# Phase buffers moved to a multiple of 256 bytes, and 353 matmuls on zeros ahead of the first projection, in a four-layer float32 network on one core

## The chip, the cores and the metric

The kernel runs on 1 core of one Trainium2 chip. The metric is the device time of one execution in microseconds. The kernel before takes 1523.93 us (median of 2 runs, 1523.18 to 1524.68).

## The reference, cut to what matters

The input x is 256 tokens by 1024 features, all in float32. Two networks run one after the other, each of two layers, and each layer is a mixer and a feed-forward part:

```python
# first network, per layer and per sandwich (mixer, then ffn)
shift, scale, gate = silu(c) @ ada_w + ada_b
h = rms_norm(x, g_pre) * (1 + scale) + shift
x = x + gate * rms_norm(fn(h), g_post)       # fn: mixer or swiglu
# mixer of layer 0: h @ hyb_w_in -> pooling and a gated scan (HGRN) -> @ hyb_w_out
# mixer of layer 1: h @ att_w_qkv -> dilated attention -> @ att_w_out
# swiglu: (silu(h @ w_a) * (h @ w_b)) @ w_out, width 2816
# second network, per layer
x = x + mixer(rms_norm(x)) @ w_out           # retention and window attention; then axial attention
x = x + square(relu(rms_norm(x) @ w_up)) @ w_down   # width 4096
```

Nearly all of the arithmetic is products of a 256-row activation with weight matrices that are read once from HBM (273 MB in all).

## The kernel before

Every product of full accuracy is made of three float32r matmuls (`three`, L1384): an operand is split into a rounded part (`hi`) and the rest (`lo`), and hi x hi, hi x lo and lo x hi are summed in one PSUM bank. Weights come in loads of 1 MB from the SyncE queue into `raw`, a ring of 6 slots. Each load is split in two halves of 128x1024. For each half ScalarE writes the rounded part to `whi` (L422) and VectorE the rest to `wlo` (L837), each a ring of 4. TensorE then runs the 24 or 48 matmuls of a half and so frees it. Its matmul instructions all go through `mm` (L1382); a weight load (PEld in the profile) goes with each.

There are three kinds of matmuls that matter here:

- `proj` of kind B and `up`: the stationary operand is a 128x128 piece of `whi` or `wlo`, the moving one 256 columns of `hhi` or `hlo`. The profile writes them `ps<-hhi,whi ... 128x256`, moving operand first.
- `proj` of kind A, and `down` for the output projections: stationary is a piece of `hhi`, `hlo`, `yhi3` or `ylo3`, moving are 512 columns of `whi` or `wlo` (`ps<-whi,hhi ... 128x512`).
- `down` in the feed-forward parts: the same, with the stationary operand a piece of `hidhi1`, `hidlo1` (first network) or `hidhi2`, `hidlo2` (second). The profile writes both pairs `hidhi` and `hidlo`.

SBUF is given out by nested stacks. First come buffers that live through the kernel (`raw`, `whi`, `wlo`, `x`, `hhi`, `hlo`, `cols`, `ident`, `ones`, ..., `small`). Behind them begin the phase buffers, sets that use the same space at different times: `ada_ring`, `acc_a` and the rest of the first network; `tmp2`, `hidhi2`, ...; `f3`, `dist`, ..., `yhi3`, `ylo3`, `qkhi`, `vhi`. In the built program the address of `raw`, `whi`, `wlo`, `hhi` and `hlo` leaves 128 when divided by 256; that of `ident` leaves 0; that of the first phase buffer, of `hidhi1`, `hidlo1`, `hidhi2` and `hidlo2` leaves 224; that of `yhi3`, `ylo3`, `qkhi` and `vhi` leaves 128, since a buffer of 32 bytes (`sinkt`) stands between them and their stack's start.

The start of the kernel, which the change touches: SyncE loads eight 1 MB pieces of `ada_w`; VectorE multiplies them with silu(c) into `acc_a` (`ada_first`, L862 and L864). TensorE runs four small matmuls on `vtab` and `voh` (bias tables) and waits for ScalarE's four copies of them (L571, L573). Then it sums `acc_a` over partitions with `ones` (`sum_cols`), transposes the normalised x (`turn`, L1491) and sums the rest. VectorE turns the sums into scale and shift (`mod_cols`, L878 to L880), makes `h` from the transposes (L936), ScalarE rounds it to `hhi` (L497), VectorE writes `hlo` (L923), and with this the first projection (`hyb_in`) begins. ScalarE's queue has the four copies of the tables ahead of its first weight splits (`split`, L422).

During `hyb_in` VectorE also works through further pieces of `ada_w`, which GpSimd's queue loads into `ada_ring`, two slots of 1 MB (L347; used at L848 and L851). A slot is loaded again once its four pieces are used. After `hyb_in` comes the scan, in eight levels (`for lv in range(NM)`): for each level TensorE waits for VectorE's masked copy of the level two before (`hg_masked`, L1065), runs `keep_warm(4)` (four products of `ident` with itself, 8 instructions), waits for VectorE's next factors (`hg_step`, L1077 to L1079) and ScalarE's copies (`hg_copied`, L625, L626), and runs 8 score products.

```python
def keep_warm(n, bank):
    for _ in range(n):
        mm(ps[:, bank, 0:P], ident[:, :], ident[:, :])
```

Of the kernel before, what the change touches and what calls it, by code (L numbers as in the profile page):

```python
# [18 lines left out]
F32 = mybir.dt.float32  # L19
F32R = mybir.dt.float32r  # L20
# [4 lines left out]
P = 128  # L25
# [54 lines left out]
even_in nr_sq nr_ssq nr_ln nr_r nr_done rp_rot rp_done  # L80
dec_step dec_ready rt_sig rt_s rt_p rt_o rt_sq rt_ssq rt_ln rt_r rt_y rt_hi rt_lo
sw_s sw_z sw_e sw_pn sw_t sw_tc sw_tl sw_o qkv_hi qkv_lo sw_sink sw_hi sw_lo
out_done dve_step act_step one_ready
""".split()


def program(nc, t):

    with ExitStack() as ctx:
        s = {name: ctx.enter_context(nc.semaphore(name)) for name in SEMS}  # L90
# [4 lines left out]
        def sb(stack, name, shape, dt=F32):  # L95
            return stack.enter_context(nc.sbuf_tensor(name, shape, dt))

        ps = ctx.enter_context(nc.psum_tensor("ps", [P, 8, 512], F32))
        raw = sb(ctx, "raw", [P, RAW, 2 * HALF])
        whi = sb(ctx, "whi", [P, 4, HALF], F32R)  # L100
# [9 lines left out]
        sc = sb(ctx, "sc", [P, KD])  # L110
        stat = sb(ctx, "stat", [P, 16])
        small = sb(ctx, "small", [P, 6, 16])


        with ExitStack() as first:
            ada_ring = sb(first, "ada_ring", [P, 2, 4, 512])
            acc_a = sb(first, "acc_a", [P, 6 * 512])
            gg = sb(first, "gg", [P, 2, D])
            grow = sb(first, "grow", [P, D])
            with ExitStack() as r:  # L120
                xn1 = sb(r, "xn1", [P, 2, D])
                h321 = sb(r, "h321", [P, 2, 512])
                vtab = sb(r, "vtab", [33, 24 + 8])
                voh = sb(r, "voh", [33, 3 * VLEN_DIL + VLEN_SWA])
                vrow = sb(r, "vrow", [8, 3 * VLEN_DIL + VLEN_SWA])
            with ExitStack() as r:
                tmp1 = sb(r, "tmp1", [P, 2, 512])
                hid1 = sb(r, "hid1", [P, 2, 512])
                acc_b = sb(r, "acc_b", [P, 2 * 512])
                hidhi1 = sb(r, "hidhi1", [P, 2, 512], F32R)  # L130
                hidlo1 = sb(r, "hidlo1", [P, 2, 512], F32R)
            with ExitStack() as r:
                f1 = sb(r, "f1", [P, 12, S])
                tok1 = sb(r, "tok1", [P, 2, 1024])
                bandqk = sb(r, "bandqk", [P, 2048])
                att1 = sb(r, "att1", [P, 8, P])
                att1o = sb(r, "att1o", [P, 4, P])
                tot2 = sb(r, "tot2", [P, 512])
                masks = sb(r, "masks", [P, NM, P])
                pooled = sb(r, "pooled", [P, 4, S])  # L140
                sq1 = sb(r, "sq1", [P, 4, S])
                poolw = sb(r, "poolw", [P, 4, P])
                y1 = sb(r, "y1", [P, 8, S])
            with ExitStack() as r:
                f2 = sb(r, "f2", [P, 24, S])
                tok2 = sb(r, "tok2", [P, 2, 1536])
                dbias = sb(r, "dbias", [P, 3, DG, S])
                prob2 = sb(r, "prob2", [P, 2, 9 * P])
                pt2 = sb(r, "pt2", [P, 9 * P])
# [188 lines left out]
        def _(pool):  # L338
# [19 lines left out]
                pool.dma_start(grow[:, :], row_of(t["norm_post"][j // 2, j % 2], D)).then_inc(s["grow_in"], 16)  # L358

            SHIFT_SCALE, GATE = [0, 512, 1024, 1536], [2048, 2560]  # L360
            pool.wait_ge(s["ada_used"], 4)
            ada_blocks(0, [(0, n) for n in GATE])
            bias_row(0)
# [457 lines left out]
        def _(dve):  # L821
# [185 lines left out]
                    body(g, 0, SPLITS.get(g, range(4)))  # L1007


            V.memset(ones[:, :], 1.0)  # L1010
            V.memset(shcol[:, :, :], 0.0)
            V.memset(small[:, 5, :], EPS).then_inc(s["one_ready"], 1)
# [367 lines left out]
        def _(pe):  # L1380
            def mm(out, lhsT, rhs, first=True, last=True):
                return pe.matmul(out, lhsT, rhs, start=first, stop=last, skip_group_check=True)  # L1382
# [165 lines left out]
                    body(g)  # L1548


            pe.wait_ge(s["const_in"], 48)
            pe.wait_ge(s["one_ready"], 1)
            for g in range(DG):
# [396 lines left out]
```

## Time and profile before

| what | value |
|---|---|
| median of 2 runs | 1523.93 us (1523.18 to 1524.68) |
| span of the profiled execution, first to last instruction | 1521.2 us |
| median less span | 2.7 us |
| TensorE busy in that span | 1416.0 us (93%), 9162 matmuls |
| VectorE, ScalarE busy | 933.2 us (61%), 706.3 us (46%) |
| mean granted TensorE clock | 0.969 of full speed |
| moved by DMA | 275.55 MB, 181 GB/s in the mean |

The profile gives the profiled execution by its span; its own time isn't listed apart, so what lies around the span is taken as median less span. Times in the rows are microseconds from the span's start. The busy time of a matmul is longer than its share of the engine, because matmuls overlap: what a matmul costs in a row of matmuls is the distance from its start to the start of the next.

### The profile page before, as it was taken

The numbers are of one execution on the slowest core, as the hardware profiler recorded it, in microseconds if no ns is written. First come the engines' busy times: TensorE is split into PE (matmuls) and PEld (weight loads), VectorE is DVE, ScalarE is ACT, GpSimd is POOL, SyncE is SP. The second block draws the span as 40 slices with busy tenths as digits, with TensorE's granted clock in tenths as the row PEclk, the third lists the DMA queues.
The fourth block names the chain that finished last, engine by engine and source line by source line (L and its number), as shares of the span: only waits on it lengthen the run. The fifth ranks groups of instructions, "written<-read, shape, count | busy, mean of one in ns | idle before, by whom it ended". The sixth has DMA issues, their size and how long they took to land.

```text
span 1521.2 us, 22829 instructions
## 1 busy us (share of the span) xinstructions
PE 1416.0 (93%) x9162; PEld 1281.7 (84%) x9162; DVE 933.2 (61%) x1155; ACT 706.3 (46%) x956; POOL 49.2 (3%) x75
## 2 busy tenths in 40 slices
PE   4898999999999998999989997899999997899998
PEld 2787899998898778999988995779998895798997
DVE  6878768875786546454465647654445548554444
ACT  2554444444444334444454646445554545445553
POOL 0100000000110000000001000000000000000000
PEclk9999899999999799999999997999999998999999
DMA  9983568985598302555546540254555540335650
GB/s 358 386 307 128 180 221 302 313 268 194 204 352 304 97 11 84 193 173 187 191 140 205 166 167 20 62 166 144 189 193 175 167 166 28 111 124 181 192 165 28
DMA packets 146049, 275.55 MB, mean 181 GB/s; under 512 B 4695, under 2 KB 83311, under 8 KB 145848
## 3 DMA queue, kind: packets, MB, share of 16 engines
q1 hardware_dynamic: 130592, 219.17, 43.1%
q0 software_dynamic: 13872, 52.05, 10.4%
q10 hardware_dynamic: 1512, 3.31, 0.6%
q8 instruction: 53, 0.87, 0.2%
q14 instruction: 20, 0.16, 0.0%
HBM read 273.40 MB, written 1.10 MB: 180 GB/s over the span
## 4 chain that ended last, share of the span: by engine, by line
PE 82%; DVE 10%; ACT 3%; DMA 3%; issue 2%; SPq 0%; DVEq 0%; ACTq 0%
PE ps L1382 80%; DVE h L936 1%; DMA raw<-in_hyb_w_in 1%; DVE wlo L837 1%; DMA ada_ring<-in_ada_w 1%; DMA raw<-in_ada_w 1%; DVE acc_a L851 1%; PE ps L1491 1%; ACT whi L422 1%; ACT pt L667 1%; DVE hlo L923 1%; DVE x L905 1%; DVE h L903 0%; ACT xn L480 0%; PE ps L1662 0%
## 5 line engine op out<-in xcount | busy, mean ns | idle before, releaser
L837 DVE TENSOR_TENSOR wlo<-raw,whi 128x1024 fp32r<-128x1024 f32 x400 | 486.3, 1224 | 443.0 <-ACT whi L422 442.6
L422 ACT CAST whi<-raw 128x1024 fp32r<-128x1024 f32 x400 | 419.3, 1050 | 606.2 <-PE ps L1382 586.9
L1382 PE MATMUL ps<-hhi,whi 128*128 128x256 f32 x1792 | 508.1, 284 | 8.1 <-DVE hlo L923 8.1
L1382 PE MATMUL ps<-hhi,wlo 128*128 128x256 f32 x1792 | 507.0, 283 | 0.0
L1382 PE MATMUL ps<-hlo,whi 128*128 128x256 f32 x1792 | 506.9, 283 | 0.0
L1382 PEld LDWEIGHTS ps<-hhi,whi 128*128 128x128 f32 x1792 | 343.3, 192 | 12.4 <-issue 10.3
L1382 PEld LDWEIGHTS ps<-hlo,whi 128*128 128x128 f32 x1792 | 343.3, 192 | 2.2 <-issue 0.2
L1382 PEld LDWEIGHTS ps<-hhi,wlo 128*128 128x128 f32 x1792 | 343.4, 192 | 0.0
L1382 PE MATMUL ps<-whi,hidhi 128*128 128x512 f32 x432 | 171.4, 397 | 0.0
L1382 PE MATMUL ps<-wlo,hidhi 128*128 128x512 f32 x432 | 171.3, 396 | 0.0
L1382 PE MATMUL ps<-whi,hidlo 128*128 128x512 f32 x432 | 171.0, 396 | 0.0
L1382 PE MATMUL ps<-whi,hhi 128*128 128x512 f32 (+1 forms) x256 | 99.0, 387 | 8.6 <-DVE hlo L923 5.2
L851 DVE SCALAR_TENSOR_TENSOR acc_a<-ada_ring,sc,acc_a 128x512 f32<-128x512 f32 (+1 forms) x126 | 94.7, 752 | 9.3 <-DMA ada_ring<-in_ada_w 4.6
L1382 PEld LDWEIGHTS ps<-whi,hidlo 128*128 128x128 f32 x432 | 81.3, 188 | 19.7
L1382 PE MATMUL ps<-whi,hlo 128*128 128x512 f32 (+1 forms) x256 | 97.0, 379 | 0.0
L1382 PE MATMUL ps<-wlo,hhi 128*128 128x512 f32 (+1 forms) x256 | 97.0, 379 | 0.0
L1382 PEld LDWEIGHTS ps<-whi,hidhi 128*128 128x128 f32 x432 | 81.5, 189 | 17.7 <-issue 0.2
L1382 PEld LDWEIGHTS ps<-wlo,hidhi 128*128 128x128 f32 x432 | 81.3, 188 | 17.7 <-issue 0.2
L1382 PE MATMUL ps<-ident 128*128 128x128 f32 x488 | 77.3, 314 | 6.7 <-DVE att L1065 6.6
L1382 PEld LDWEIGHTS ps<-ident 128*128 128x128 f32 x488 | 72.2, 228 | 9.0 <-DVE att L1065 7.5
L1382 PEld LDWEIGHTS ps<-whi,hhi 128*128 128x128 f32 x256 | 48.7, 190 | 19.3 <-issue 7.7
L1382 PEld LDWEIGHTS ps<-wlo,hhi 128*128 128x128 f32 x256 | 48.8, 191 | 9.3 <-issue 0.7
(213 smaller groups left out, 1281.0 us busy)
## 6 DMA issues: line engine op xcount, KB each, us to landing
raw<-in_ffn_w_in SPq DMA_DIRECT2D x44, 1024.0 KB, 5.3
ada_ring<-in_ada_w POOLq DMA_DIRECT2D x40, 1024.0 KB, 6.8
raw<-in_w_mlp_up SPq DMA_DIRECT2D x32, 1024.0 KB, 5.5
raw<-in_w_mlp_down SPq DMA_DIRECT2D x32, 1024.0 KB, 5.0
raw<-in_ffn_w_out SPq DMA_DIRECT2D x22, 1024.0 KB, 5.0
raw<-in_att_w_qkv SPq DMA_DIRECT2D x18, 1024.0 KB, 6.0
raw<-in_w_in_even SPq DMA_DIRECT2D x18, 1024.0 KB, 5.1
raw<-in_hyb_w_in SPq DMA_DIRECT2D x10, 1024.0 KB, 15.0
```

The lines of the kernel that those rows point to most:

```text
L422: A.copy(whi[:, H % 4, :], raw[:, slot(n), h * HALF:(h + 1) * HALF]).then_inc(s["hi_ready"], 1)
L667: A.copy(pt2[:, a:a + n], flat(bank)[:, 0:n] if tt else ps[:, 5, 0:n]).then_inc(s["dl_tc"], 1)
L837: V.tensor_tensor(wlo[:, H % 4, :], raw[:, slot(n), h * HALF:(h + 1) * HALF], whi[:, H % 4, :].bitcast(F32), ALU.subtract).then_inc(s["lo_ ...
L851: ins = V.scalar_tensor_tensor(out=out, in0=ada_ring[:, kh, kk, :], scalar=sc[:, k:k + 1], in1=out, op0=ALU.mult, op1=ALU.add)
L905: V.scalar_tensor_tensor(out=x[:, tt, :], in0=h, scalar=stat[:, 2 + tt:3 + tt], in1=x[:, tt, :], op0=ALU.mult, op1=ALU.add).then_inc(s["x_ ...
L923: V.tensor_tensor(hlo[:, 2 * q:2 * q + 2, :].rearrange("p a b -> p (a b)"), h32[:, q % 2, :], hhi[:, 2 * q:2 * q + 2, :].rearrange("p a b ...
L936: ins = V.tensor_scalar(h32[:, q % 2, kk * S:(kk + 1) * S], ps[:, q, kk * S:(kk + 1) * S], scol[:, j, k:k + 1], shcol[:, j, k:k + 1], ALU. ...
L1382: return pe.matmul(out, lhsT, rhs, start=first, stop=last, skip_group_check=True)
L1491: m = pe.transpose(ps[:, k // 2, (k % 2) * S + tt * P:(k % 2) * S + (tt + 1) * P], xn[:, tt, k * P:(k + 1) * P], ident[:, :])
```

## The change

Three things are done.

1. An unused buffer of 32 bytes (`pad1`) stands behind `small`. Every phase buffer moves up by 32 bytes. In the built program the first phase buffer, `hidhi1`, `hidlo1`, `hidhi2`, `hidlo2`, `f1` to `f3` and `tok1` to `tok3` now leave 0 when divided by 256. `yhi3`, `ylo3`, `qkhi` and `vhi` go from 128 to 160. `raw`, `whi`, `wlo`, `hhi`, `hlo` and `ident` stay where they are.
2. VectorE clears 1024 columns of `whi`, all 2048 of `hhi` and half of a new buffer `warm` (3072 of 6144 columns, at an address that leaves 128) ahead of its other work; GpSimd clears the other half of `warm` ahead of its first wait.
3. TensorE waits for both and runs, ahead of the table matmuls, 25 sets of float32r matmuls on these zeros: one set of 40 and 24 of 12, each with another offset of the stationary operand (in elements of 4 bytes), of the moving operand, of their width or of their number of PSUM banks. Each set ends with a matmul of 64 columns.

```diff
         small = sb(ctx, "small", [P, 6, 16])
+        sb(ctx, "pad1", [P, 8])
...
                 vrow = sb(r, "vrow", [8, 3 * VLEN_DIL + VLEN_SWA])
+                sb(r, "pad2", [P, 64])
+                warm = sb(r, "warm", [P, 6144], F32R)
...
             SHIFT_SCALE, GATE = [0, 512, 1024, 1536], [2048, 2560]
+            pool.memset(warm[:, 3072:6144].bitcast(F32), 0.0).then_inc(s["warm_ready"], 1)
             pool.wait_ge(s["ada_used"], 4)
...
+            V.memset(whi[:, 0, :].bitcast(F32), 0.0)
+            V.memset(hhi[:, :, :].bitcast(F32), 0.0)
+            V.memset(warm[:, 0:3072].bitcast(F32), 0.0).then_inc(s["warm_ready"], 1)
             V.memset(ones[:, :], 1.0)
...
+            pe.wait_ge(s["warm_ready"], 2)
+            hw, ww = hhi[:, :, :].rearrange("p a b -> p (a b)"), whi[:, 0, :]
+            def warm_up(n, a, b, width, outs):
+                for i in range(n):
+                    o = outs[i % len(outs)]
+                    mm(ps[:, o[0], o[1]:o[1] + width], a[i % len(a)], b[i % len(b)][:, 0:width])
+                mm(ps[:, 3, 0:64], ww[:, 0:128], hw[:, 0:64])
...
+            def SS(off):
+                return [at(ww, 128 * i + off, 128) for i in range(7)]
+            def HH(off, n=256):
+                return [at(hw, n * i + off, n) for i in range(3)]
+            W8 = [at(warm, 128 * i, 128) for i in range(8)]
+            W5 = [at(warm, 2048 + 512 * i, 512) for i in range(4)]
+            warm_up(40, SS(0), HH(0), 256, one)
...
+            warm_up(12, SS(96), HH(0), 256, four)
...
+            warm_up(12, SS(96), HH(96, 512), 512, four)
...
             pe.wait_ge(s["const_in"], 48)
```

TensorE's instructions at the program's start, before (`vtab` and `voh` are the bias tables, `ones` with `acc_a` the column sums, `xn1` the normalised x):

```order
L1382 MATMUL ps<-voh,vtab 8x384 x3
L1382 MATMUL ps<-voh,vtab 8x512
L1382 MATMUL ps<-ones,acc_a 128x1 x8
L1491 MATMUL ps<-ident,xn1 128x128 x16
L1382 MATMUL ps<-ones,acc_a 128x1 x8
L1382 MATMUL ps<-whi,hhi 128x512
```

The same place of the changed kernel, the first sets and the last two with what follows (the sets between them are left out):

```order
L1389 MATMUL ps<-hhi,whi 128x256 x40
L1389 MATMUL ps<-hhi,whi 128x64
L1389 MATMUL ps<-hhi,whi 128x256 x12
...
L1389 MATMUL ps<-hhi,warm 128x128 x12
L1389 MATMUL ps<-hhi,whi 128x64
L1389 MATMUL ps<-voh,vtab 8x384 x3
L1389 MATMUL ps<-voh,vtab 8x512
L1389 MATMUL ps<-ones,acc_a 128x1 x8
```

Of the added matmuls 244 are 256 columns wide (40 and 17 sets of 12), 72 are 512 wide, 12 are 128 wide and 25 are 64 wide. They stand ahead of the first thing that TensorE did, and nothing else moved on it.

VectorE's first instructions in the changed kernel (in the one before they begin with the third row from the end of these, the clearing of `ones`):

```order
L1014 MEMSET whi 128x1024
L1015 MEMSET hhi 128x2048
L1016 MEMSET warm 128x3072
L1017 MEMSET ones 128x128
L1018 MEMSET shcol 128x64
L1019 MEMSET small 128x16
```

The three new rows stand ahead of the one that releases ScalarE's first norms (`one_ready`) and of the first use of `ada_w`. On the other engines the order of the instructions is the same, but for GpSimd's one clearing.

## Rows read from the trace of the kernel before

**Rows 1.** The page: busy time, and the chain that ended last.

```profile
PE 1416.0 (93%) x9162; PEld 1281.7 (84%) x9162; DVE 933.2 (61%) x1155; ACT 706.3 (46%) x956; POOL 49.2 (3%) x75
PE 82%; DVE 10%; ACT 3%; DMA 3%; issue 2%; SPq 0%; DVEq 0%; ACTq 0%
```

**Rows 2.** Timeline, TensorE from the start: start, length, what, idle before.

```profile
13.99 5.71 PE L1382 MATMUL ps<-voh,vtab 33*8 33x384 f32 x8 [13.99 <-DMA voh<-in_voh]
20.37 3.72 PE L1382 MATMUL ps<-ones,acc_a 128*128 128x1 f32 x16 [0.67 <-ACT vrow L573]
25.89 3.68 PE L1491 MATMUL ps<-ident,xn 128*128 128x128 f32 x16 [1.81 <-DVE xn L914]
44.29 0.77 PE L1382 MATMUL ps<-whi,hhi 128*128 128x512 f32 x1 [5.25 <-DVE hlo L923]
44.86 0.63 PE L1382 MATMUL ps<-wlo,hhi 128*128 128x512 f32 x1
...
48.27 0.52 PE L1382 MATMUL ps<-whi,hhi 128*128 128x512 f32 x1
```

**Rows 3.** Timeline, VectorE and ScalarE from the start.

```profile
0.84 0.17 DVE L1010 MEMSET ones<- 128x128 f32 x1 [0.84 <-PEq L1937]
6.59 0.49 DVE L862 TENSOR_SCALAR acc_a<-raw,sc 128x512 f32<-128x512 f32 x1 [1.48 <-DMA raw<-in_ada_w]
12.69 3.12 DVE L864 SCALAR_TENSOR_TENSOR acc_a<-raw,sc,acc_a 128x512 f32<-128x512 f32 x4 [3.24 <-DMA raw<-in_ada_w]
19.74 0.58 ACT L573 COPY vrow<-ps 8x512 f32<-8x512 f32 x1 [1.24 <-PE ps L1382]
41.18 0.16 DVE L878 TENSOR_TENSOR shcol<-ps,cols 128x8 f32<-128x8 f32 x1
103.50 0.91 DVE L1053 MEMSET att<- 128x1024 f32 x1 [0.16 <-issue]
```

**Rows 4.** Timeline, TensorE: a `down`'s 1st matmul, what follows its 24th, and the 29th after.

```profile
209.76 0.39 PE L1382 MATMUL ps<-whi,hidhi 128*128 128x512 f32 x1
...
215.37 0.28 PE L1382 MATMUL ps<-hhi,whi 128*128 128x256 f32 x1
...
218.84 0.28 PE L1382 MATMUL ps<-hhi,wlo 128*128 128x256 f32 x1
```

**Rows 5.** Timeline, TensorE: 24 matmuls of the output projection on `yhi3` and `ylo3`.

```profile
991.04 0.39 PE L1382 MATMUL ps<-whi,yhi 128*128 128x512 f32 x1
...
996.48 0.39 PE L1382 MATMUL ps<-whi,yhi 128*128 128x512 f32 x1
```

**Rows 6.** Groups by line and shape: count, busy time and mean ns.

```profile
L1382 PE MATMUL ps<-whi,hidhi 128*128 128x512 f32 x432 | 171.4, 397 | 0.0
L1382 PE MATMUL ps<-whi,yhi 128*128 128x512 f32 x32 | 12.4, 389 | 0.0
```

**Rows 7.** Timeline, VectorE, ScalarE and TensorE, 86 to 124 us.

```profile
86.92 0.49 DVE L848 TENSOR_SCALAR acc_a<-ada_ring,sc 128x512 f32<-128x512 f32 x1 [4.12 <-DMA ada_ring<-in_ada_w]
92.07 3.11 DVE L851 SCALAR_TENSOR_TENSOR acc_a<-ada_ring,sc,acc_a 128x512 f32<-128x512 f32 x4 [2.30 <-DMA ada_ring<-in_ada_w]
113.90 0.66 ACT L625 COPY pooled<-bandqk 128x512 f32<-128x512 f32 x1
118.16 2.08 PE L1382 MATMUL ps<-ident 128*128 128x128 f32 x8 [5.84 <-DVE att L1065]
120.03 3.62 PE L1382 MATMUL ps<-pooled,sq 128*128 128x128 f32 x16
124.44 1.95 PE L1382 MATMUL ps<-bandqk 128*128 128x128 f32 x16
```

**Rows 8.** Busy time by stretch: PE, PEld, DVE, ACT, POOL, then clock, DMA share, GB/s.

```profile
80.00:90.00 10.00, 10.00 (x48) 8.50 (x48) 4.64 (x6) 7.83 (x8) 0.00 (x0) 1.00 1.03 399
118.00:124.00 6.00, 5.84 (x29) 5.84 (x30) 3.17 (x6) 1.39 (x3) 0.00 (x0) 0.53 0.70 231
124.00:130.00 6.00, 5.33 (x46) 4.95 (x44) 6.00 (x9) 2.49 (x5) 0.00 (x0) 1.00 0.00 0
```

More of the change, by code:

```diff
@@ L82 @@
 sw_s sw_z sw_e sw_pn sw_t sw_tc sw_tl sw_o qkv_hi qkv_lo sw_sink sw_hi sw_lo
-out_done dve_step act_step one_ready
+out_done dve_step act_step one_ready warm_ready
 """.split()
@@ L1548, in mlp, with at @@
                     body(g)
+            pe.wait_ge(s["warm_ready"], 2)
[5 more added lines that the diff above has]
+                mm(ps[:, 3, 0:64], ww[:, 0:128], hw[:, 0:64])
+            def at(src, off, n):
+                return src[:, off:off + n]
+            one, two, four = [(0, 0)], [(0, 0), (1, 0)], [(0, 0), (1, 0), (2, 0), (3, 0)]
+            def SS(off):
[5 more added lines that the diff above has]
+            warm_up(40, SS(0), HH(0), 256, one)
+            warm_up(12, SS(0), HH(0), 256, one)
+            warm_up(12, SS(0), HH(0), 256, four)
+            warm_up(12, SS(0), HH(0)[:1], 256, four)
+            warm_up(12, SS(0)[:1], HH(0), 256, four)
+            warm_up(12, SS(96), HH(0), 256, four)
+            warm_up(12, SS(32), HH(0), 256, four)
+            warm_up(12, SS(16), HH(0), 256, four)
+            warm_up(12, SS(8), HH(0), 256, four)
+            warm_up(12, SS(4), HH(0), 256, four)
+            warm_up(12, SS(2), HH(0), 256, four)
+            warm_up(12, SS(96), HH(96), 256, four)
+            warm_up(12, SS(96), HH(32), 256, four)
+            warm_up(12, SS(96), HH(16), 256, four)
+            warm_up(12, SS(96), HH(8), 256, four)
+            warm_up(12, SS(96), HH(4), 256, four)
+            warm_up(12, SS(96), HH(0, 512), 512, four)
+            warm_up(12, SS(96), HH(96, 512), 512, four)
+            warm_up(12, SS(8), HH(0, 512), 512, four)
+            warm_up(12, SS(96), W5, 512, four)
+            warm_up(12, W8, W5, 512, four)
+            warm_up(12, W8, HH(96), 256, four)
+            warm_up(12, W8, [w[:, 0:256] for w in W5], 256, four)
+            warm_up(12, SS(96)[:1], HH(96, 512)[:1], 512, four)
+            warm_up(12, W8, HH(96), 128, four)
             pe.wait_ge(s["const_in"], 48)
```

## The prediction

> **What bounds the kernel now.** I read the page first: TensorE is busy for 93% of the span and stands for 82% of the chain that ended last [rows 1]. So a microsecond that TensorE gains or loses anywhere in its steady stages is one of the kernel's. Then the timeline of the first 50 us [rows 2, 3]: TensorE's real work begins only at 44.29; before it runs 56 small matmuls and waits for `ada_w` and VectorE. That is where the new matmuls are put, so the question is how much of them fits there. Then the distance between matmul starts in steady stretches, by operand [rows 4 to 6], since the move of the buffers can change nothing but that. Last the stretch up to 124 us, where VectorE and DMA and not TensorE set the pace for a while [rows 7, 8].
>
> **The pace of matmuls by operand.** In a feed-forward `down`, 24 matmuls of 512 columns take 215.37 - 209.76 = 5.61 us, 234 ns each; stationary is `hidhi` or `hidlo`, at 224 over a multiple of 256 [rows 4]. In the output projection 24 matmuls with the same moving buffers, banks and order take 996.48 - 991.04 = 5.44 us, 227 ns each; stationary is `yhi3` or `ylo3`, at 128 [rows 5]. The one difference that I see is the stationary operand's address. It even shows in the busy times, 397 ns against 389 [rows 6]. The 256-wide ones with both operands at 128 take 218.84 - 215.37 = 3.47 us for 29 [rows 4], 120 ns.
>
> **Part 1, the move by 32 bytes.** `hidhi` stands in 432 + 432 matmuls and `hidlo` in 432: 1296 in all (one of three rows with the same count stands in [rows 6]). They go from 224 to 0. No row has a float32r matmul with its stationary operand at 0. If 0 is as good as 128, each gains 5.61/24 - 5.44/24 = 7.1 ns: 1296 x 7.1 = 9.2 us. The bounds: the gain may be nothing, and it may be larger, for even at 227 ns a matmul is 14 ns above its 512 columns at 2.4 GHz (213 ns); all of that gone would be 1296 x 21 = 27 us. On the other side a relation of 0 to the moving operand's 128 could be worse than 224 to 128; from the nearest rows I give that the same 7 ns, 9 us. I take -9.2, the row that I have. `yhi3` and `ylo3` go from 128 to 160, in 96 matmuls (3 x 32): if 160 is as bad as 224, +0.7 us. The rest (`qkhi`, `vhi`, VectorE's and ScalarE's operands) I cost at nothing; those matmuls stand among waits on other engines.
>
> The Trainium skill (SBUF — State Buffer, Specifications) gives lines of 16 bytes as what costs when crossed. Both 224 and 0 are multiples of 16, so by that rule the move would be worth nothing; the pair 234 and 227 ns speaks against it, as both of those addresses are multiples too. It is the first rival below. The same skill (TensorE: Matmul & The Clock Gate, Back-to-back issue gap) gives N/2.4 + 2.5 ns for a warm matmul, 216 ns at 512, which no float32r row here reaches; by it the upper bound would be 1296 x 18 = 23 us.
>
> **Part 2, the clearing.** VectorE's 1024 columns of zeros took 0.91 us [rows 3], so 6144 columns are 5.4 us, and it is done at 0.84 + 5.4 = 6.3. Its first `ada_w` piece then starts at about 8 and not 6.59; the wait of 3.24 us before 12.69 [rows 3] swallows this. GpSimd's 3072 columns lie beside it; no row shows its clearing at this size, between 2.7 us (VectorE's rate) and, as an estimate, three times that, 8 us. Its first DMA waited for `ada_used` until 22 us anyway. TensorE starts its sets at 6.5 (up to 8.5).
>
> **Part 3, the sets.** Cold, a 512-wide matmul took 0.426 us (44.86 to 48.27, eight of them) [rows 2], so a 256-wide one is 0.213. The clock rose about 4 us after the projection's start, for the matmul at 48.27 is the first shorter one (0.52). I take 4 us cold here too (19 matmuls). The other 225 of 256 columns: 225 x 0.120 = 27.0. 72 of 512 at 0.227 to 0.234: 16.6. The 37 of 128 or 64 columns are not shown in float32r; between 0.06 us each (columns alone) and 0.21 (cold), I take 0.11, about a weight load: 4.1. Sum 4 + 27.0 + 16.6 + 4.1 = 51.7 us (bounds 46 to 60), to 58.2. Nothing hides beneath it: all of TensorE's start work is queued behind. And ScalarE's first splits stand behind its copies of the tables, which wait for TensorE.
>
> Behind the sets all inputs have landed, and the clock is up. Table matmuls 5.71 us at half clock [rows 2], now 2.9; ScalarE's last copy 0.6 [rows 3]; 16 sums, 16 transposes and 16 sums (8 and 8) at half of 3.7 each [rows 2]: 5.5. Together 9.0, to 67.2. Then from the scale and shift (41.18, rows 3) to the first projection (44.29) 3.1, and 0.3 for the hand-over: 70.6. ScalarE's first four splits run during the sums. **The projection starts 26.3 us later.**
>
> **What comes back.** (a) The projection's first 4.0 us ran at 0.426 instead of 0.227 us: 1.9 us lost before. With TensorE idle for only 3 us and not 5.25 beforehand it should start warm: -1.9 (bounds 0 and -1.9). (b) In the kernel before VectorE waited 4.12 + 2.30 us for `ada_ring`, whose DMAs stood among the weight loads [rows 7] while the queues moved 399 GB/s at full share [rows 8]. VectorE then was late for the scan: TensorE idled 5.84 us before 118.16, and its clock was 0.53 in the 6 us behind [rows 8], so that the 24 matmuls (8 from 118.16, 16 from 120.03, end 123.65) took twice as long as at full clock. After the change the two `ada_ring` loads and six weight loads have landed long before the projection, so the DMA queues are empty when the next are issued. What is late next is ScalarE: its copies for level 1 (113.90, done 115.1 with the second) release level 2, which before began its 16 products at 120.03 and cold. I reckon level 3 (124.44) comes 5 us earlier relative to the projection. Bounds 0 (VectorE late anyway) and -6.4 (all its wait). -5.0.
>
> **Sum** against the profiled span of 1521.2: + 26.3 - 1.9 - 5.0 - 9.2 + 0.7 = + 10.9, to 1532.1. Median less span was 2.7 us, so the time is 1534.8; I say 1534.5.
>
> **Rivals.**
> 1. *The new address of the hidden buffers is worth nothing* (the change doesn't do what it says): what slows them is their relation to the moving operand at 128, and 0 is no better than 224. For it: no row shows a stationary operand at 0. Against: 128 is good, and 0 is the rounder number. Then 26.3 - 6.9 = + 19.4 and no loss on `yhi3`: 1543.
> 2. *0 is better than 128.* The 14 ns above the columns, which `whi` and `hhi` pay at 128, fall away with the stationary operand at 0. For it: those 14 ns ask for a cause, and the stationary address has been seen to move the pace. Against: `whi` as moving operand stays at 128, and may be what costs them. Then 1296 x 21 = 27 in place of 9.2: + 10.9 - 18 = - 7: 1517; half of it 1526.
> 3. *The sets run at half clock throughout, and the kernel is slower by more than 2%* (2% is 30.5 us, about what a measurement of this kernel can tell from no change). Zeros in both operands might not count as work, or the clock may rise late. Then the sets take 244 x 0.213 + 72 x 0.427 + 37 x 0.11 = 86.8 us, 35 more, the small matmuls behind them 8 more: 1534.5 + 43 = 1577. It decides from where the sets take over 51.7 + 20 = 72 us. Against it: `ident` holds zeros in all but one of 128 places, and the clock was 1.0 from 124 to 130 us, where `keep_warm` is a third of the matmuls [rows 8]. A GpSimd clearing of over 25 us would have the same end.
>
> **How the numbers follow.** Forecast 0.57; rival 1 0.20; rival 2 0.15; rival 3 0.08. Cases 1 and 2 with the bounds of the start (- 4 to + 10) and of what comes back (0 to - 8.3) span 1517 to 1553; the range is 1519 to 1553 and leaves out rival 3 and the end of rival 2. Faster by over 2% needs 41 us less than forecast, which no bound gives: 0.01. Slower by over 2% (above 1554.4) is rival 3 and the sum of all bad ends: 0.09. The rest, within 2%: 0.90.
>
> **What would show it.** The first weight split after the sets and the first projection at 70 to 71 us; the sets ending at 58; matmuls on `whi` and `hidhi` at 227 ns and not 234 (24 in 5.44 us), those on `yhi3` at 234; 256-wide ones unchanged at 120; VectorE without a wait for `ada_ring` in the projection, and a gap of TensorE before level 2 of the scan of 2 us and not 5.84. A set that takes over 4 us cold, a pace of 234 or of 215 on `hidhi`, or a gap that stays would each show its own step wrong.

## The result: 1549.87 us, slower by 1.7%

The changed kernel takes 1549.87 us (median of 2 runs, 1549.83 to 1549.9) where the kernel before takes 1523.93: a ratio of 1.0171, interval 1.0141 to 1.02. That is 25.9 us more; the forecast was 10.6 more. The measured time lies inside the predicted range, but the forecast has less than half of the loss. The profiled execution has a span of 1548.1 us and a mean granted clock of 0.971.

The page of the changed kernel, the two lines that answer to [rows 1]:

```profile
PE 1455.6 (94%) x9515; PEld 1321.4 (85%) x9515; DVE 938.8 (61%) x1158; ACT 705.5 (46%) x956; POOL 51.9 (3%) x76
PE 82%; DVE 11%; ACT 4%; issue 2%; DMA 1%; POOL 0%; DVEq 0%; ACTq 0%
```

TensorE has 353 more matmuls and 39.6 us more busy time, and it is as much of the chain as before. DMA's share of the chain fell from 3% to 1%: this is the start, where `ada_w` is no longer waited for.

The timeline of TensorE's start in the changed kernel (start, length, what, idle before), which answers to [rows 2]; the projection's first matmul is the one at 74.20:

```profile
7.35 38.37 PE L1389 MATMUL ps<-hhi,whi 128*128 128x256 f32 x275 [7.35 <-DVE warm L1016]
...
58.81 2.96 PE L1389 MATMUL ps<-voh,vtab 33*8 33x384 f32 x8
62.43 3.58 PE L1389 MATMUL ps<-ones,acc_a 128*128 128x1 f32 x16 [0.66 <-ACT vrow L577]
65.87 3.49 PE L1498 MATMUL ps<-ident,xn 128*128 128x128 f32 x16
69.20 1.84 PE L1389 MATMUL ps<-ones,acc_a 128*128 128x1 f32 x16
74.20 0.77 PE L1389 MATMUL ps<-whi,hhi 128*128 128x512 f32 x1 [3.16 <-DVE hlo L927]
...
79.03 0.52 PE L1389 MATMUL ps<-whi,hlo 128*128 128x512 f32 x1
```

The sets fill 7.35 to 58.81 us. The first of them run at half clock: behind the very first the starts stand 213 ns apart up to 11.0 us, 3.7 us in all, and then 116 to 121 ns. (The trace's record of the clock begins only there.) Then the 16 first sums and the 16 transposes take 3.4 us each, nearly as long as at the start of the kernel before, though nothing but a gap of 0.66 us separates them from 51 us of dense work; only the last 16 sums run at full pace. The projection starts at 74.20 and not at 44.29, 29.9 us later. Its first matmuls stand 0.43 us apart again: the first shorter one is at 79.03.

The busy time by stretch shows why (PE, PEld, DVE, ACT and POOL busy, granted clock, DMA share, GB/s):

```profile
62.50:69.30 6.80, 6.80 (x34) 6.80 (x34) 2.36 (x2) 3.88 (x4) 0.00 (x0) 0.52 0.29 60
74.20:79.10 4.90, 4.90 (x12) 3.88 (x13) 4.70 (x8) 2.18 (x4) 0.00 (x0) 0.50 0.22 59
```

In both stretches TensorE is busy without a gap and is granted 0.5 of its clock (1.2 of 2.4 GHz).

The next view is VectorE's timeline at the scan's inputs, and then TensorE's at levels 2 and 3; it answers to [rows 7]:

```profile
114.81 0.49 DVE L852 TENSOR_SCALAR acc_a<-ada_ring,sc 128x512 f32<-128x512 f32 x1 [1.71 <-DMA ada_ring<-in_ada_w]
119.82 3.12 DVE L855 SCALAR_TENSOR_TENSOR acc_a<-ada_ring,sc,acc_a 128x512 f32<-128x512 f32 x4 [2.15 <-DMA ada_ring<-in_ada_w]
```

```profile
145.90 1.16 PE L1389 MATMUL ps<-ident 128*128 128x128 f32 x8 [3.45 <-DVE att L1072]
146.89 1.95 PE L1389 MATMUL ps<-pooled,sq 128*128 128x128 f32 x16
149.63 1.95 PE L1389 MATMUL ps<-bandqk 128*128 128x128 f32 x16
```

VectorE still waits for `ada_ring`, but 3.9 us and not 6.4. TensorE idles 3.45 us before level 2 and not 5.84, and its 8 and 16 matmuls run at full clock (1.16 and 1.95 us, before 2.08 and 3.62). Level 3 starts 25.2 us later than in [rows 7]: of the 29.9 that the start cost and the 0.5 that the projection's cold stretch is longer, 5.2 came back. How much of this is the change's doing is taken up below, with the prediction's term.

Last, the pace. The timeline of TensorE in a feed-forward `down` of the changed kernel (24 matmuls between the two rows, as in [rows 4]), and in the output projection (24 between the rows, as in [rows 5]):

```profile
235.32 0.39 PE L1389 MATMUL ps<-whi,hidhi 128*128 128x512 f32 x1
...
240.90 0.28 PE L1389 MATMUL ps<-hhi,whi 128*128 128x256 f32 x1
...
1017.48 0.39 PE L1389 MATMUL ps<-whi,yhi 128*128 128x512 f32 x1
...
1023.07 0.40 PE L1389 MATMUL ps<-whi,yhi 128*128 128x512 f32 x1
```

The hidden buffers at 0 give 5.58/24 = 232.5 ns, not the 227 that was forecast (before 234). `yhi3` and `ylo3` at 160 give 5.59/24 = 232.9 ns where they had 227. So the address mattered in both places, and 0 is not a good one. The group's mean busy time says it more weakly, 395 ns where [rows 6] has 397:

```profile
L1389 PE MATMUL ps<-whi,hidhi 128*128 128x512 f32 x432 | 170.7, 395 | 0.0
```

### The profile page after: what moved, and what is told of

It is laid out like the page before. It is cut to its first block, busy times and chain, and to the rows that moved or that the text cites. A ratio compares the mean times of both kernels' runs of the same rounds, so it can differ in the third digit from the quotient of the medians.

```text
span 1548.1 us, 23539 instructions
## 1 busy us (share of the span) xinstructions
PE 1455.6 (94%) x9515; PEld 1321.4 (85%) x9515; DVE 938.8 (61%) x1158; ACT 705.5 (46%) x956; POOL 51.9 (3%) x76
## 4 chain that ended last, share of the span: by engine, by line
PE 82%; DVE 11%; ACT 4%; issue 2%; DMA 1%; POOL 0%; DVEq 0%; ACTq 0%
PE ps L1389 81%; DVE h L940 1%; DVE wlo L841 1%; DVE acc_a L855 1%; PE ps L1498 1%; DMA ada_ring<-in_ada_w 1%; ACT whi L426 1%; DVE x L909 1%; DVE hlo L927 1%; DVE h L907 1%; ACT pt L671 1%; ACT xn L484 0%; PE ps L1716 0%; DVE small L1306 0%; ACT rs L454 0%
## 5 line engine op out<-in xcount | busy, mean ns | idle before, releaser
L1389 PE MATMUL ps<-hhi,whi 128*128 128x256 f32 (+2 forms) x2085 | 551.5, 287 | 20.8 <-DVE hlo L927 12.9
L1389 PEld LDWEIGHTS ps<-hhi,whi 128*128 128x128 f32 x2085 | 384.2, 193 | 27.2 <-issue 15.6
L1389 PE MATMUL ps<-ident 128*128 128x128 f32 x488 | 71.3, 297 | 4.3 <-DVE att L1072 4.2
L1389 PEld LDWEIGHTS ps<-ident 128*128 128x128 f32 x488 | 65.9, 211 | 6.6 <-DVE att L1072 5.1
```

## The experiments

Theory A through all of them: what sets the pace of a float32r matmul is the *difference* of the stationary and the moving operand's addresses modulo 256, and not the stationary operand's own. The hidden buffers had the difference 224 - 128 = 96 and got 0 - 128, which is 128. The good difference for 512 columns would be 0. In all kernels the whole reference is computed; they differ in where buffers lie and in matmuls on zeros. "Before" is the kernel before on the same chip.

### The two halves of the change apart

The move alone:

```diff
# the kernel before
+        sb(ctx, "pad1", [P, 8])
```

> The kernel before with the 32-byte move alone, no clearing and no matmuls on zeros. Theory A (what counts is the stationary operand's address relative to the moving one's, and only an equal remainder by 256 gives 227 ns at 512 columns): in the changed kernel hidhi at 0 against whi at 128 ran at about 232.6 ns, so 1296 x 1.6 ns = 2 us are gained and 96 x 6 ns = 0.6 us lost: 1.4 us faster, about 1522.5. Rival B (the move costs time through VectorE, ScalarE or DMA on the phase buffers, and this is part of the 26 us): slower than 1524, by 5 us or more. The forecast on record would have had it at 1515.4.

Measured: 1520.19 us (10 runs) against 1524.39; ratio 0.9975, interval 0.9965 to 0.9984. The pace on the hidden buffers is 232.3 ns in the mean and on `yhi3` 233. The move is a small gain, 4.2 us, more than the 1.6 of the paces (1296 x 1.7 ns less 96 x 6). The spans of the two profiled executions differ by 2.3. What the gain holds beyond the paces stays open; the ten runs go from 1518.83 us at a mean granted clock of 0.974 to 1523.26 at 0.965.

The sets alone:

```diff
# the changed kernel
-        sb(ctx, "pad1", [P, 8])
```

> The changed kernel without the 32-byte buffer: the matmuls on zeros and the clearing alone. Theory A: 29.9 us later at the first projection, about 3 to 5 us back at the scan, nothing from the move: 1549.9 + 1.4 = 1551, 27 us over before. Rival B: 1545 or less. The first projection starts at 74.2 in either.

Measured: 1556.45 us (4 runs) against 1524.39; ratio 1.0209, interval 1.0189 to 1.0229. Expected was +27, measured +32: a miss of 5 us. The projection starts at 74.70, as expected; all of the sums and transposes but the last few run at half clock. The mean granted clock of the trace is 0.963, where the whole change has 0.971, and of the 7.6 us between the two spans the paces explain 1.6. Why the clock is lower in this kernel was not tried. With the move's -4.2 the two halves sum to +27.9, and the whole change measured +25.9. So the loss is the sets', and its centre is the start. Each half carries some microseconds that neither account explains.

### Theory A: the difference of the addresses

In the kernel before, the hidden buffers are put at 128 over a multiple of 256, where the moving operand is too:

```diff
# the kernel before
+                sb(r, "padh1", [P, 40])
                 hidhi1 = sb(r, ...
...
+            sb(r, "padh2", [P, 40])
             hidhi2 = sb(r, ...
```

> The kernel before with 160 bytes ahead of hidhi1 and hidhi2 alone, so that the hidden buffers leave 128, as whi and wlo do. Theory A: 1296 matmuls from 234.2 to 226.7 ns, 9.7 us faster: 1514.2. Rival C (the hidden matmuls are slow from something else than their address, such as the engine's other traffic in the feed-forward parts): stays at 234 or 232 ns, 1522 to 1524.

Measured: 1516.26 us (4 runs), ratio 0.9953, interval 0.9936 to 0.9969; 8.1 us faster, which is what the prediction had put down for the move. The same place as [rows 4], 24 matmuls in the timeline of TensorE:

```profile
208.50 0.40 PE L1384 MATMUL ps<-whi,hidhi 128*128 128x512 f32 x1
...
213.97 0.28 PE L1384 MATMUL ps<-hhi,whi 128*128 128x256 f32 x1
```

5.47/24 = 227.9 ns: 128 is good for these buffers and 0 is not. This alone doesn't tell the own address from the difference, as only the stationary operand was moved. A kernel that measures the pace by itself replaces the sets with 16 sets of 21, in which the stationary operand's offset goes through 0, 32, ..., 224 bytes while the moving one stays:

```diff
# the changed kernel, in place of the 24 sets of 12
+            for off in (0, 8, 16, 24, 32, 40, 48, 56):
+                warm_up(21, SS(off), HH(0), 256, four)
+            for off in (0, 8, 16, 24, 32, 40, 48, 56):
+                warm_up(21, SS(off), HH(0, 512), 512, four)
```

> The changed kernel with other sets: 40 of 256 columns, then 8 sets of 21 of 256 and 8 of 512 columns, with the stationary operand 0, 32, 64, 96, 128, 160, 192 and 224 bytes past the moving one by the remainder of 256, which stays at 128. Theory A: at 512 columns 227 ns at 0, 233 to 234 at 32, 96, 128; at 256 columns 120 at 0 and 113 at 64, as in the changed kernel's sets; unknown are 160, 192, 224 and 512 columns at 64. If the law is symmetrical, 192 is as 64 and 224 as 32; if it goes by 128, 192 is as 64 and 128 as 0, which the changed kernel already speaks against.

Measured (median distance of starts in a set, ns; difference is stationary less moving, modulo 256 bytes):

| difference | 0 | 32 | 64 | 96 | 128 | 160 | 192 | 224 |
|---|---|---|---|---|---|---|---|---|
| 256 columns | 120 | 118 | 113.5 | 117 | 120 | 120 | 118 | 118 |
| 512 columns | 227 | 233 | 233 | 233 | 232 | 232 | 229 | 234 |

The timeline of TensorE in this kernel, cut to pieces of single sets: 256 columns at the differences 0 and 64, 512 columns at 0 and 32:

```profile
15.28 1.84 PE L1389 MATMUL ps<-hhi,whi 128*128 128x256 f32 x14
...
20.25 1.86 PE L1389 MATMUL ps<-hhi,whi 128*128 128x256 f32 x15
...
37.00 2.67 PE L1389 MATMUL ps<-hhi,whi 128*128 128x512 f32 x11
...
41.69 2.96 PE L1389 MATMUL ps<-hhi,whi 128*128 128x512 f32 x12
```

The length of a row runs to the end of its last matmul, which is busy 0.28 or 0.39 us. So the first is 13 distances in 1.84 - 0.28 = 1.56 us, 120 ns, and the second 14 in 1.58, 113 ns; the others are 10 in 2.28, 228 ns, and 11 in 2.57, 233 ns. At 512 columns equal remainders are best, as theory A says, and both 96 (before) and 128 (after) are bad. At 256 columns, which are 5376 of the kernel's matmuls, equal remainders are among the *worst* (120 ns, as at 128 and 160), and 64 is the best.

That the difference decides, and not the stationary operand's own address, is seen in sets of the changed kernel. At 512 columns, with the stationary operand at 0 in both, the pace settles at 226 to 227 ns when the moving one is at 0 too (`SS(96)` with `HH(96, 512)`), and goes between 228 and 241 when it is at 128 (`SS(96)` with `HH(0, 512)`). With the same stationary operand 256 columns run at 112 to 123 ns when the moving one is at 128 (120 in the table), and at 113 to 114 when it is at 192, the same as the stationary one at 192 with the moving one at 128. In the last two pairs the difference is 64. Their offsets from the buffers' starts differ by 384 and 320 bytes, and these behave as 128 and 64 do, so only the remainder by 256 is seen to count.

### Using it: the weights 64 bytes past the activations

To part the weights from `hhi` by 64 bytes they have to stand behind it. First the new order of the buffers alone, with all remainders as in the kernel with the hidden buffers at 128:

```diff
# the kernel before, with padh1 and padh2 of 40
-        whi, wlo, x, hhi, hlo
+        hhi, hlo, x, whi, wlo
```

> The same new order of the buffers without the 64 bytes: every address's remainder is as in the run with the hidden buffers at 128. Theory A: 1516, the same within 0.2%. Rival E (the order, and so which region of SBUF a buffer lies in, matters for pace): differs from 1516 by more than 5 us.

Measured: 1515.28 us (4 runs) against 1524.22; ratio 0.9943, interval 0.9926 to 0.9959. The gain is 8.9 us here and 8.1 with the old order, and the two intervals overlap: no effect of the order is seen, with the same remainders.

```diff
# the one above
         x = sb(ctx, "x", [P, 2, D])
+        sb(ctx, "padw", [P, 16])
         whi = sb(ctx, "whi", [P, 4, HALF], F32R)
```

> The kernel before with the weight rings laid 64 bytes past the activations (order raw, hhi, hlo, x, 64 bytes, whi, wlo), and the hidden buffers at the weights' remainder (192). Theory A, the relation of stationary to moving address sets the pace, with the table that the probe gave: 256-column matmuls with whi or wlo stationary 64 bytes past hhi run at 113.4 ns and not 120 (5376 x 6.6 ns = 35 us), those of 512 columns with hhi stationary stand at 192 and cost 229 and not 227 (672 x 2.5 = 2 us lost), the hidden ones at 0 run at 227 (9 us): about 1482, or up to 1490 where DMA or VectorE sets the pace in the first and the qkv projections. Rival D (the relation holds for zeros and short sets alone): 120 ns stays, 1516.

Measured: 1501.87 us (4 runs), ratio 0.9853, interval 0.9836 to 0.9869. The expectation of 1482 to 1490 was missed: the gain over the reordered kernel is 13.4 us and not 25 or more. The place of [rows 4] again:

```profile
208.36 0.40 PE L1385 MATMUL ps<-whi,hidhi 128*128 128x512 f32 x1
...
213.82 0.28 PE L1385 MATMUL ps<-hhi,whi 128*128 128x256 f32 x1
...
217.24 0.28 PE L1385 MATMUL ps<-hhi,wlo 128*128 128x256 f32 x1
```

29 matmuls of 256 columns take 3.42 us, 117.9 ns, where the probe has 113.5. The same operands run at two paces: at full clock the 256-wide ones have a mean of 116.6 ns, with the lowest tenth at 113 and the highest at 118. Taken run by run it is one or the other: all 46 runs that begin right behind a hidden `down` keep 117.8, while among others the longest run (575 distances, from 389 us, behind an idle time) keeps 113.4. The hidden ones keep their 227, since moving and stationary both moved.

If the difference has a sign, the weights 64 bytes *before* the activations (192) should be worth less:

```diff
# the kernel before, with padh1 and padh2 of 24
+        sb(ctx, "padw", [P, 16])
         x = sb(ctx, "x", [P, 2, D])
```

> The kernel before with 64 bytes between wlo and x, so that hhi and hlo stand at 192 and the weights at 128 (the stationary weights 64 bytes before the moving operand), and the hidden buffers at the weights' 128. Theory A with its sign: 256-column matmuls at the probe's 118 (relation 192), 11 us gained; hidden ones 9 us gained; 672 with hhi stationary are now 64 past the moving weights and cost 233 to 234, 5 us lost, and yhi3 0.6 lost: 1509 to 1510, between the two kernels with the hidden buffers moved (1516) and the weights 64 past (1502). If the sign doesn't matter, it is 1502 too.

Measured: 1509.03 us (4 runs) against 1524.78; ratio 0.9897, interval 0.988 to 0.9914. The 256-wide ones run at 117.7 ns in the mean, those with `hhi` or `yhi3` as stationary operand at 233. This fell as expected. Against the kernel with the hidden buffers at 128: 5376 x 2.2 ns = 11.8 us less, 768 x 6 ns = 4.6 us more, 7.2 measured.

### Why 118 and not 113

A second kernel of sets: in each 12 matmuls of 512 columns, with both operands at the same remainder, then 48 of 256 in the order that `three` has, at the differences 0, 48, 56, 64, 72, 80 and 192:

```diff
# the changed kernel, in place of the 24 sets of 12
+            for off in (0, 12, 14, 16, 18, 20, 48):
+                mixed(off, three_order)
```

> The changed kernel with 7 other sets after the 40: each 12 matmuls of 512 columns with equal remainders, then 48 of 256 columns in the order of three (two with one stationary operand, one with another), the stationary operand 0, 48, 56, 64, 72, 80 and 192 bytes past the moving one. In the run with the weights 64 bytes past, the 256-column matmuls behind hidden ones ran at 117.7 ns and not at the probe's 113.4. If it is what ran before them (512-column matmuls set the phase), the set at 64 stays at 117 to 118 for its 48 here too. If it is something of the real kernel (ScalarE's and VectorE's traffic, data that isn't zero), it goes to 113.4. Another distance than 64 may hold 113.

Measured, in ns: 120.0, 123.3, 117.7, 117.8, 118.3, 119.0 and 117.8 in the mean of the last part of each set. At 64 the pace is 117.8 for all 48 matmuls, with no other engine's work on these buffers. The timeline of TensorE in this set:

```profile
43.78 5.35 PE L1389 MATMUL ps<-hhi,whi 128*128 128x256 f32 x44
```

43 distances in 5.35 - 0.28 = 5.07 us are 118 ns. In the other kernel of sets a run at 64 reached 113 within six matmuls; it stood right behind one 64-column matmul, but it had another order of operands too, so the pair of kernels doesn't settle what decides. That the same addresses have two steady paces is seen; that what ran before decides which is tried next. Ahead of each run of 256-wide matmuls one of 64 columns is put:

```diff
# the kernel with the weights 64 bytes past
+                    if nudge and h == 0:
+                        mm(ps[:, bank, 0:64], wh[:, 0, 0:P], hhi[:, 0, 0:64])
```

(and likewise in the projections of kind B; 62 in all. The bank is cleared by the next matmul's start.)

> The kernel with the weights 64 bytes past, and one matmul of 64 columns ahead of each run of 256-column matmuls (into the bank that the run's first matmul starts anew). In the probes a set at 64 bytes behind such a matmul went to 113.4 ns after some five matmuls, and one behind 512-column matmuls stayed at 117.8. If the start of a run decides it, the 256-column matmuls go to 113.4 and, less some 120 ns per nudge and about 70 of these, 10 to 15 us are gained on 1502. If not, 1502 to 1510.

Measured: 1497.99 us (4 runs) against 1523.49; ratio 0.9827, interval 0.9803 to 0.985. Timeline of TensorE at the same place, the two matmuls behind the last hidden ones (one is the added one), the fourth after them, and one 23 later:

```profile
214.34 0.39 PE L1385 MATMUL ps<-hhi,whi 128*128 128x64 f32 x2
214.58 0.28 PE L1385 MATMUL ps<-hlo,whi 128*128 128x256 f32 x1
...
215.05 0.28 PE L1385 MATMUL ps<-hhi,wlo 128*128 128x256 f32 x1
...
217.65 0.28 PE L1385 MATMUL ps<-hlo,whi 128*128 128x256 f32 x1
```

From 215.05 to 217.65 there are 23 matmuls, 113.0 ns each. Of the 62 added matmuls 47 stand right behind 512-wide ones, and behind all 47 the pace is 113.3. As nothing but the added matmul is new ahead of these runs, what ran before does decide the pace.

But of the 10 to 15 us expected only 3.9 came. In the whole kernel the mean at full clock goes from 116.6 to 115.3 only, and all 256-wide matmuls together, transitions included, take 7 us less (624 against 631); the added ones themselves cost 2.7. One reason is that the first matmul behind an added one takes about 87 ns longer. The other is that an added matmul can tip the pace the wrong way. Six of them fell into the middle of a stretch that ran at 113.3, and behind all six it ran at 117.8; in three of these places (586, 830 and 1198 us) the kernel without them stays at 113.3. Of three that fell into a stretch at 117.8, two turned it to 113.3. TensorE's timeline at the first of these (five distances of starts from the first row to the second, 15 from the third to the last):

```profile
196.87 0.28 PE L1385 MATMUL ps<-hlo,whi 128*128 128x256 f32 x1
...
197.44 0.39 PE L1385 MATMUL ps<-hhi,whi 128*128 128x64 f32 x2
197.67 0.28 PE L1385 MATMUL ps<-hlo,whi 128*128 128x256 f32 x1
...
199.44 0.28 PE L1385 MATMUL ps<-hlo,whi 128*128 128x256 f32 x1
```

Ahead of it 0.57/5 = 114 ns, behind it 1.77/15 = 118 ns. So the matmul seems to belong behind the 512-wide ones alone; that kernel was not run. This kernel is the fastest of all that ran, 26 us better than the one before and 52 better than the changed one.

### The start

Only the first 9 sets of the changed kernel:

```diff
# the changed kernel
-            warm_up(12, SS(8), HH(0), 256, four)
...
-            warm_up(12, W8, HH(96), 128, four)
```

> The changed kernel with the first 9 of the 25 sets alone (136 matmuls, of 256 columns, ending at about 26 us). Theory A: the column sums then reach their wait for ada_w at about 37 us as before, so the sets are free, the projection starts at 44.3 to 45, and the time is that of the move alone, 1520 to 1522. Rival F (the sets cost their own length wherever they end, since something else waits for them, as the clearing or ScalarE's copies): 18 us over it, 1540.

Measured: 1520.39 us (7 runs) against 1524.22; ratio 0.9976, interval 0.9964 to 0.9987: the same as with the move alone (0.9975). Timeline of TensorE:

```profile
26.49 2.96 PE L1389 MATMUL ps<-voh,vtab 33*8 33x384 f32 x8
30.11 1.95 PE L1389 MATMUL ps<-ones,acc_a 128*128 128x1 f32 x16 [0.66 <-ACT vrow L577]
31.92 3.55 PE L1498 MATMUL ps<-ident,xn 128*128 128x128 f32 x16
35.27 1.04 PE L1389 MATMUL ps<-ones,acc_a 128*128 128x1 f32 x8
38.89 1.86 PE L1389 MATMUL ps<-ones,acc_a 128*128 128x1 f32 x8 [2.58 <-DVE acc_a L868]
44.92 0.77 PE L1389 MATMUL ps<-whi,hhi 128*128 128x512 f32 x1 [4.16 <-DVE hlo L927]
```

The sets end at 26.49, there is still a wait of 2.58 us for VectorE's `acc_a`, and the projection starts at 44.92, 0.6 later than before. So 19 us of matmuls on zeros were free: they lie beneath the loading of `ada_w`. Sets that end within this cover cost nothing that the time shows, and neither does the clearing.

The full change with 28 products of `ident` ahead of the projection, to keep the clock up over VectorE's last steps:

```diff
# the changed kernel
+            keep_warm(14, 7)
             proj("hyb_in", HYB[0:3], j=0)
```

> The changed kernel with 28 products of ident with itself between the last column sum (71.0 us) and the first projection (74.2). They fill the 3.2 us of idle time. If the clock fell at 72.8 because TensorE stood idle, the projection's first 5 us run at full clock and it gains 2.5 us: 1547.4. If the clock falls for what went before (the small matmuls from 58.8 on), nothing is gained: 1550.

Measured: 1552.21 us (4 runs) against 1524.22; ratio 1.0178, interval 1.0156 to 1.02. No gain. Timeline of TensorE:

```profile
69.38 3.41 PE L1389 MATMUL ps<-ones,acc_a 128*128 128x1 f32 x16
72.65 5.93 PE L1389 MATMUL ps<-ident 128*128 128x128 f32 x28
78.34 0.48 PE L1389 MATMUL ps<-whi,hhi 128*128 128x512 f32 x1
78.65 0.40 PE L1389 MATMUL ps<-wlo,hhi 128*128 128x512 f32 x1
```

The projection does start at nearly full pace, and so saves about the 2.4 us that its cold stretch costs. But the last sums and the 28 products ran at half clock, 5.93 us for 28 (212 ns each), and ended some 2.5 us after the inputs were ready (VectorE's first `hlo` was written at 75.8); the projection started at 78.34 and not at 74.20, which costs more than was saved. In this trace the clock is 0.50 already from 69.4 to 72.6 us, while TensorE is busy with the last sums, where the changed kernel has 1.00 from 69.3 to 71.1; so there was no full clock that the products could keep up. Whether the idle time or the small matmuls ahead of it lowered the changed kernel's clock is not settled by this, and fewer products, that end with the wait, were not tried.

## Why the prediction was wrong

**The move (-9.2), the step that failed most.** It measured about -2.2 (1296 matmuls from 234.0 to 232.3 ns; their distances of under 400 ns, 1294 in each trace, sum to 302.8 and 300.6 us). The rows showed 224 bad and 128 good with the moving operand at 128 in both. The prediction named the stationary operand's own address as the one difference and took 0 to be as good as 128. It is the relation to the moving operand that counts: 227 ns at 512 columns with both operands at 0, both at 128 and both at 192, and 232 in the changed kernel's pair of 0 and 128. Rival 1 had said this: at 0.20, with 1543. Of that rival its mechanism held and its "no loss on `yhi3`" didn't (96 x 6 ns, +0.6, as the forecast had it). The sum had listed a bound for "a relation of 0 to 128 that could be worse", and could have seen that 0 and 224 are both off the moving operand's 128. Rival 2 (0 better than 128) is out. This term is 7.0 of the miss of 16.0 us (the spans: +26.9 against +10.9).

**The small matmuls behind the sets (9.0 us).** Tables 2.96 (2.9 said) and ScalarE's last copy came as said. The 16 sums, 16 transposes and 16 sums took 62.43 to 71.04, 8.6 us, and not 5.5: the step took the clock to stay up after the sets, and the granted clock was 0.52 from 62.5 to 69.3. That is +3.1; the later end of the sets adds 0.6, so that the projection is at 74.20 and not 70.6, +3.6. The forecast had no row of such matmuls at full clock right behind dense work, and took one outcome without a bound for the other, which [rows 2] would have given.

The Trainium skill (TensorE: Matmul & The Clock Gate) ties the clock to TensorE's activity. The trace agrees for idle time (below: behind 3.01 us of it the clock is 1.00, behind 4.92 us 0.50); in the stretch from 62.5 to 69.3 TensorE is busy for 6.80 of 6.80 us and the clock is at half nonetheless, so a TensorE that the profile shows busy can still be at half clock.

**The projection's warm start (-1.9).** It didn't come; the clock was 0.50 from 74.2 to 79.1, and the cold stretch lasted 4.9 us instead of 4.0. +2.4 against the sum.

**The sets (51.7 us, from 6.5 to 58.2).** 51.46 measured, from 7.35 to 58.81. Right; the cold part was 3.7 us where 4 were taken. The late start is VectorE's: `hhi` and `warm` took 1.76 and 2.62 us as reckoned, with gaps of 0.38 and 0.59 us between the clearings that the step left out:

```profile
1.04 0.91 DVE L1014 MEMSET whi<- 128x1024 f32 x1 [1.04 <-PEq L1991]
2.32 1.76 DVE L1015 MEMSET hhi<- 128x2048 f32 x1 [0.38 <-issue]
4.68 2.62 DVE L1016 MEMSET warm<- 128x3072 f32 x1 [0.59 <-issue]
```

GpSimd's clearing had an unknown cost, bounded at 2.7 to 8 us; it is 2.66:

```profile
0.75 2.66 POOL L364 MEMSET warm<- 128x3072 f32 x1 [0.29 <-POOLq L1991]
```

**The scan (-5.0).** -5.2, right in size. What it was put down to is there: fewer waits of VectorE, a shorter gap, a warm level 2; only the gap is 3.45 and not 2, since 3.9 us of VectorE's 6.4 stayed. But that the early loads are the cause isn't shown, and luck may be in the size. From the first matmul of the projection to level 3 the kernel before takes 80.2 us (124.44 - 44.29) and the changed one 75.4, the longer cold stretch included. The trace of the move alone, where nothing is loaded early, takes 76.6, with waits for `ada_ring` of 2.31 and 2.16 us and a gap of 4.06; with the hidden buffers at 128 alone it is 78.7, and with the sets alone 78.0. There is one trace of each kernel, so between 1.5 and 3.6 of the 5.2 us may be what this stretch does by itself.

**What the sum did not have.** From level 3 to the end the changed kernel should have come back another 1.6 us by its paces (-2.2 + 0.6), and instead went from +25.2 to +26.9: 3.3 us lost. The distance of the two traces changes by jumps, up as well as down. In the changed kernel's times it grows by 2.1 us at 419.3, by 1.6 at 929.7 and by 1.0 at 1282, each time where the changed kernel has the lower clock; by 0.8 at 832.38, where the clock is full in both and TensorE waits 0.59 us for VectorE's `wlo`; and by 0.4 near 212. It shrinks by 0.6 ahead of 419, by 1.3 up to 541, by 0.4 near 818 and by 0.5 up to 976, where the kernel before has the lower clock. Together that is 3.1 of the 3.3. Windows of the changed kernel, and the same work in the kernel before:

```profile
419.30:423.60 4.30, 4.28 (x20) 4.30 (x21) 1.94 (x2) 0.00 (x0) 0.55 (x1) 0.50 0.17 53
930.20:932.50 2.30, 2.30 (x7) 1.83 (x6) 0.69 (x1) 0.00 (x0) 0.00 (x0) 0.50 0.85 232
```

```profile
394.70:397.10 2.40, 2.38 (x20) 2.40 (x21) 1.93 (x2) 0.00 (x0) 0.13 (x1) 1.00 0.06 16
904.30:906.60 2.30, 2.30 (x12) 1.77 (x11) 1.38 (x2) 0.00 (x0) 0.00 (x0) 1.00 0.59 153
```

The first is the start of a feed-forward part: 20 matmuls in 4.3 us, before in 2.4, 1.9 us. Ahead of it TensorE idled longer:

```profile
419.32 0.55 PE L1389 MATMUL ps<-hhi,whi 128*128 128x256 f32 x1 [4.92 <-DVE hlo L927]
```

In the kernel before this gap is 3.01 us (its first matmul is at 394.72), and in the one with the move alone 4.95, with a cold start too. Over ten kernels it goes together: behind 3.01 to 3.04 us of idle time the 20 matmuls take 2.4 to 2.5 us (five kernels), behind 4.10 us 3.7 to 3.8 (two), behind 4.92 to 4.95 us 4.4 (three). TensorE reached the place earlier, and VectorE's chain, which doesn't depend on TensorE's clock, did not; so time gained ahead of the gap was paid back behind it. In the second pair of windows the kernel before gets through 12 matmuls where the changed one gets through 7. That these clock dips, and one wait, are the rest of the miss is read from one trace of each kernel; why the chip grants one stretch and not another was not tried. It also sets how finely any of these kernels can be told apart: the mean granted clock is 0.969 in the trace before, 0.971 after, 0.963 with the sets alone and 0.975 in the reordered one.

In sum: 7.0 (the move) + 3.6 (the start) + 2.4 (the projection's clock) - 0.2 (the scan) - 0.1 (`yhi3`) + 3.3 (later clock, and the wait for `wlo`) = 16.0 us, the miss. Rival 3, sets at half clock, did not occur: the sets were cold for their first few us only.

## What to carry to other kernels

Before a matmul's pace is blamed on an address, compare the *pair*: 120, 118 and 113 ns at 256 columns, and 227 and 233 at 512, came from the same instructions with another difference of the two operands modulo 256 bytes, and another order of the buffers with three paddings made the kernel before 1.5% faster. Work added ahead of everything is free only up to the first thing that it delays: here 19 us of it cost nothing, and 51 us put the first projection off by 30. And a saving ahead of a wait for another engine can lower the clock behind it, so count what comes back, not what was taken away.

## What the hardware showed that was not expected

- The pace of a float32r matmul depends on the stationary less the moving address modulo 256 bytes, and the best difference isn't the same at both widths: 0 at 512 columns (227 ns; 229 at 192 and 232 to 234 elsewhere), 64 at 256 columns (113.5 in short sets; 120 at 0, 128 and 160). A difference of +64 is not one of -64 (113.5 and 118). The cause is open.
- With the difference at 64 there are two steady paces, 113.3 and 117.8 ns. Which one a run takes hangs on what ran before: right behind the 512-wide matmuls of a hidden `down` it was 117.8 in 46 of 46 runs, and behind 512-wide ones 113.3 in 47 of 47 with a single matmul of 64 columns between, at some 90 ns for the next one. Put into the middle of a stretch at 113.3, the same matmul turned it to 117.8 in 6 of 6. The cause is open.
- TensorE's granted clock was 0.52 over 6.8 us in which it was busy throughout, with sums of one column and transposes, right behind 51 us of dense matmuls at full clock.
- The Trainium skill (SBUF — State Buffer, Specifications) names lines of 16 bytes as what costs when crossed. All offsets in the table above are multiples of 32, and still the pace spans 113 to 120 ns, so that rule doesn't account for it.
